# Building the experts' diagonal matrices on ScalarE instead of VectorE in a hybrid attention, DeltaNet and PEER block

## What is computed

```python
def peer(h, w_query, keys1, keys2, expert_down, expert_up):
    ...
        top_s, pos = lax.top_k(cand, PEER_TOPK)                 # 16 experts per head
        eidx = jnp.take_along_axis(cidx, pos, axis=-1)
        gates = jax.nn.softmax(top_s, axis=-1)
        u = expert_down[eidx]
        act = jax.nn.gelu(jnp.einsum('td,thkd->thk', xb, u).astype(jnp.float32), approximate=False)
        ve = expert_up[eidx]
        return jnp.einsum('thk,thkd->td', (gates * act).astype(xb.dtype), ve)
```

## Time and profile before

| | |
|---|---|
| device time, three runs | 2172.28, 2175.07, 2176.78 us; median 2175.07 |
| span of the profiled execution | 2172.1 us |
| before the first expert's dot | 0 to 493.5 us |
| experts of tiles 0 and 1, woven with the front | 493.5 to 1428.3 us |
| experts of tiles 2 and 3, alone | 1428.3 to 2154.7 us |
| busy: PE, DVE, ACT, POOL | 80%, 66%, 26%, 55% |
| moved from HBM | 649.84 MB |

### The profile page before, as it was taken

How to read it: one execution, slowest core, us unless ns; L and a number is a source line. 1 busy time by engine, 2 the same in 40 slices (tenths; PEclk the granted TensorE clock), 3 DMA queues, 4 the chain that set the end, 5 groups by cost and what they waited for, 6 DMA issues and landing times. The chain is left out here.

```text
span 2172.1 us, 23919 instructions
## 1 busy us (share of the span) xinstructions
PE 1742.9 (80%) x6788; PEld 1122.4 (52%) x6788; DVE 1431.1 (66%) x3407; ACT 558.1 (26%) x1222; POOL 1191.0 (55%) x1060
## 2 busy tenths in 40 slices
PE   7999999976878798787899868857777766777775
PEld 7888888864555475555666636522223322222222
DVE  0523322037788878888878787877677768677675
ACT  1522221021355427512333031121111111112111
POOL 2000000007656577566577667667777776777775
PEclk8999999988989899898999989989988997889988
DMA  8443234429989798788899999999999998999996
GB/s 295 130 139 119 79 117 136 146 87 355 399 280 330 281 407 316 250 299 275 294 409 394 408 326 404 379 344 366 368 358 365 382 366 333 371 368 371 360 380 242
DMA packets 178360, 653.16 MB, mean 301 GB/s; under 512 B 20096, under 2 KB 20304, under 8 KB 177504
## 3 DMA queue, kind: packets, MB, share of 16 engines
q0 software_dynamic: 148112, 541.77, 66.9%
q1 hardware_dynamic: 29952, 109.20, 14.5%
q10 hardware_dynamic: 208, 1.08, 0.1%
HBM read 649.84 MB, written 2.10 MB: 300 GB/s over the span
## 5 line engine op out<-in xcount | busy, mean ns | idle before, releaser
L1767 PE MATMUL PS<-pool_e,diag 128*128 128x512 f32 x1408 | 752.6, 677 | 324.9 <-DVE diag L1327 320.2
L589 POOL DMA_INDIRECT pool_e<-in_peer_u,idx x384 | 479.3, 1248 | 742.5 <-DVE idx L1306 473.2
L1767 PEld LDWEIGHTS PS<-pool_e,diag 128*128 128x128 f32 x1408 | 281.3, 212 | 710.2 <-issue 365.3
L589 POOL DMA_INDIRECT pool_e<-in_peer_v,idx x448 | 480.7, 1073 | 155.9 <-issue 125.6
L1350 DVE SCALAR_TENSOR_TENSOR pool_e<-pool_e,H 128x1024 f32<-128x1024 f32 x384 | 469.4, 1223 | 109.9 <-DMA pool_e<-in_peer_u,idx 97.9
L1481 PE MATMUL PS<-hT,ring 128*128 128x256 f32 x1792 | 407.1, 386 | 3.3 <-ACT hT L881 3.3
L1481 PEld LDWEIGHTS PS<-hT,ring 128*128 128x128 f32 x1792 | 348.3, 195 | 76.2 <-issue 29.7
L903 ACT ACTIVATE acts<-dots 128x1 f32<-128x1 f32 x256 | 51.4, 203 | 608.6 <-DVE pool_e L1350 299.6
L1327 DVE TENSOR_SCALAR diag<-ident,acts,wts 128x128 f32<-128x128 f32 x416 | 140.9, 345 | 3.7 <-ACT acts L909 3.6
L1350 DVE SCALAR_TENSOR_TENSOR gT<-gT,H 128x1024 f32<-128x1024 f32 x64 | 78.4, 1225 | 78.3 <-DMA gT<-in_peer_u,idx 77.1
L909 ACT ACT_TABLE_LOAD x59 | 75.7, 1283 | 184.5 <-DVE pool_e L1350 184.4
(11 more groups left out here) (323 smaller groups left out, 1907.0 us busy)
## 6 DMA issues: line engine op xcount, KB each, us to landing
ring<-in_w_tiles SPq DMA_DIRECT2D x200, 512.0 KB, 4.5
pool_e<-in_peer_v,idx POOLq DMA_INDIRECT x448, 6.3
pool_e<-in_peer_u,idx POOLq DMA_INDIRECT x384, 6.5
hT<-in_x_cols SPq DMA_DIRECT2D x2, 1024.0 KB, 8.3
mods<-in_ada_rows POOLq DMA_DIRECT2D x1, 2048.0 KB, 11.5
out_x<-X SPq DMA_DIRECT2D x4, 512.0 KB, 6.5
scores<-in_gain_rows POOLq DMA_DIRECT2D x1, 1536.0 KB, 15.9
X<-in_x_rows POOLq DMA_DIRECT2D x1, 1024.0 KB, 19.1
```

Of the source, the lines that this page charges most:

```text
L589: pool.indirect_dma_start(out=slot, out_offset=None, in_=table, in_offset=bass.IndirectOffsetOnAxis(ap=idx_sb[p][:, k:k + 1], axis=0),).th ...
L1767: ins = pe.matmul(PS[:, BANK_Y + half, :], diag[:, tile, :], rows[:, half * S:(half + 1) * S], start=False, stop=False, skip_group_check=True)
```

## The change

ACT makes the diagonal matrix. It applies gelu to (identity x dot), with the dot as a scale per token, and writes all 128x128 numbers into `diag` (gelu of 0 is 0, so only the diagonal remains); a second ACT instruction multiplies the matrix by the gate in place. For the experts that DVE adds up, ACT also makes the product of gelu and gate, one column at a time. DVE's `weigh` and the product in `add_up` are gone. Two semaphores are new: `wts_ready` (DVE to ACT: the gates of a head) and `act_ready` (ACT to DVE: the products). The wait for a free `diag` buffer (`e_free`) moves from DVE to ACT.

```diff
-LAG = (2, 2)
+LAG = 2
...
-            def gelu(head, p, k):
+            def gelu_of(p, k, tile):
+
+                act.activation(diag[:, tile, :], ident[:, :], ACT.Gelu, scale=dots[p][:, k:k + 1]).then_inc(gelu_ready, 1)
+
+            def gated_by(p, k, tile):
+
+                act.mul(diag[:, tile, :], diag[:, tile, :], wts[p][:, k:k + 1]).then_inc(diag_ready, 1)
+
+            def weigh_pair(h, k):
+
+                if k % 2 == 0:
+                    return
+                p = h % 2
+                if k == 1:
+                    act.wait_ge(wts_ready, h + 1)
+                for j in (k - 1, k):
+                    n = h * TOPK + j
+                    act.wait_ge(dot_ready, n + 1)
+                    if not added_by_pe(n):
+                        act.activation(acts[p][:, j:j + 1], dots[p][:, j:j + 1], ACT.Gelu).then_inc(gelu_ready, 1)
+                    else:
+                        m = count_pe(n)
+                        if m >= NDG:
+                            act.wait_ge(e_free, m + 1 - NDG)
+                        gelu_of(p, j, m % NDG)
+                for j in (k - 1, k):
+                    n = h * TOPK + j
+                    act.wait_ge(gelu_ready, n + 1)
+                    if added_by_pe(n):
+                        gated_by(p, j, count_pe(n) % NDG)
+                    else:
+                        act.mul(acts[p][:, j:j + 1], acts[p][:, j:j + 1], wts[p][:, j:j + 1]).then_inc(act_ready, 1)
+
+            def weigh(head, p, k):
+
                 act.wait_ge(dot_ready, head * TOPK + (k + 1))
-                act.activation(acts[p][:, k:k + 1], dots[p][:, k:k + 1], ACT.Gelu).then_inc(gelu_ready, 1)
-
-            def gelu_pair(h, k):
-
-                if k % 2:
-                    act.wait_ge(dot_ready, h * TOPK + k + 1)
-                    act.activation(acts[h % 2][:, k - 1:k + 1], dots[h % 2][:, k - 1:k + 1],
-                                   ACT.Gelu).then_inc(gelu_ready, 2)
+                act.wait_ge(e_free, head * TOPK + (k + 1 - NDG + LATER))
+                gelu_of(p, k, k % NDG)
+                act.wait_ge(gelu_ready, head * TOPK + (k + 1))
+                gated_by(p, k, k % NDG)
...
-                "expert": gelu_pair,
+                "expert": weigh_pair,
...
+                        act.wait_ge(wts_ready, head + 1)
+                        act.sem_inc(seen_act, 1)
                         for k in range(TOPK):
-                            gelu(head, p, k)
+                            weigh(head, p, k)
...
                 dve.tensor_scalar(wts[p][:, :], gate[p][:, 0:TOPK], gate[p][:, TOPK + 2:TOPK + 3], None,
-                                  ALU.mult)
+                                  ALU.mult).then_inc(wts_ready, 1)
                 dve.drain()
-
-            def weigh(head, p, k):
-
-                dve.wait_ge(gelu_ready, head * TOPK + (k + 1))
-                m = count_pe(head * TOPK + k) if isinstance(head, int) else k
-                if not isinstance(head, int):
-
-                    dve.wait_ge(e_free, head * TOPK + (k + 1 - NDG + LATER))
-                elif m >= NDG:
-                    dve.wait_ge(e_free, m + 1 - NDG)
-                dve.tensor_scalar(diag[:, m % NDG, :], ident[:, :], acts[p][:, k:k + 1],
-                                  wts[p][:, k:k + 1], ALU.mult, ALU.mult).then_inc(diag_ready, 1)
 
             def add_up(h, p, k):
...
-                dve.wait_ge(gelu_ready, n + 1)
-                link(dve.tensor_tensor(out=acts[p][:, k:k + 1], in0=acts[p][:, k:k + 1], in1=wts[p][:, k:k + 1],
-                                       op=ALU.mult))
+                dve.wait_ge(act_ready, n + 1 - count_pe(n + 1))
...
-                for m in behind(n, LAG[0]):
-                    (weigh if added_by_pe(m) else add_up)(m // TOPK, m // TOPK % 2, m % TOPK)
+                for m in behind(n, LAG):
+                    if not added_by_pe(m):
+                        add_up(m // TOPK, m // TOPK % 2, m % TOPK)
...
                             dot(p, k, u_slots[1][slot], h2)
-                            if k >= LAG[1]:
-                                weigh(head, p, k - LAG[1])
                             if k % 3 == 0 and k // 3 < 4:
 
                                 choose(1, ahead % HEADS if p else ahead, 1 - p, k // 3)
-                        for k in range(TOPK - LAG[1], TOPK):
-                            weigh(head, p, k)
```

More of the change, by code:

```diff
@@ L431, in hybrid_block @@
         gelu_ready = sem("gelu_ready")
+        act_ready = sem("act_ready")
+        wts_ready = sem("wts_ready")
         diag_ready = sem("diag_ready")
```

## The result

| | before | after |
|---|---|---|
| device time, median of 20 runs each | 2174.18 us | 2168.72 us (2148.11 to 2178.67) |
| ratio, 95% interval | | 0.9957 (0.9939 to 0.9976) |
| span of the profiled execution | 2172.1 us | 2168.3 us |
| first stretch (tiles 0 and 1, with the front), first dot to first dot | 934.8 us | 919.0 us |
| second stretch (tiles 2 and 3), first dot to last dot | 725.1 us | 737.7 us |

The change makes the kernel faster by 5.5 us, 0.4%, where 40 us were forecast; the time lies just above the range of 2095 to 2168. The direction was right and the size was not. The two stretches moved against each other: 15.8 us gained in the first, 12.6 us lost in the second.

The account below looks back on a forecast made before the run. POOL's queue of gathers was taken to bound the second stretch; DVE, row supply or ACT, by head, the first. Terms -25 - 9 + 4 + 4 - 5.5 - 9 = -40.5 gave 2135 us, range 2095 to 2168.

Parts of the forecast that it names:

- Starts of tiles: Second stretch, two tiles: ACT makes expert 0's matrix 2.8 us sooner, so PE starts earlier; -5.5 us.
- Table loads ahead of the wait: First stretch: ACT's table load moves before its wait for a dot, shortening the chain 0.85 us at 11 places; -9 us.
- DVE's relief: First stretch: 56.5 us of matrices and products leave DVE's queue, part of it kept; -25 us, bounds 0 and -56.
- the seven heads where DVE leads: First stretch: about seven of 16 heads (convolutions, DeltaNet, modulation before the scores) where DVE was said to set the pace.
- ACT's own work: First stretch: ACT's added instructions lengthen attention by 4 us and DeltaNet by 4 us; bounds for both 0 and +16.
- First stretch in all: First stretch: DVE's relief, Table loads ahead of the wait and ACT's own work taken together; -26 us.
- Gathers held by dots: Second stretch: without matrices between dots, 60 gathers that follow a held one run 0.15 us shorter; -9 us.
- Second stretch: Tiles 2 and 3: Starts of tiles and Gathers held by dots taken together; -14.5 us.
- signs of failure: Forecast wrong if DVE's or PE's waits for ACT pass 50 us, second stretch changes over 25, or first stays unchanged.
- Supply bound everywhere: Rival, both stretches: rows of u come no sooner however early buffers are free; 2166 us, chance 0.15.
- ScalarE becomes the bound: Rival, heads 5 to 9: ACT's added work delays PE's next stage and outweighs the relief; 2191 us, chance 0.10.
- The matrices held the gathers: Rival, second stretch: DVE's matrices cause the 86 us of held gathers; 2081 us, chance 0.09 shared with full relief kept.

Follow-up runs that it names:

- e8: Kernel before, with the first stretch's gelu of two columns split into two of one column, each with its own wait; 2165.9 us, ratio 0.9962.
- e9: Kernel before, with VectorE's 160 matrices and 96 products of the first stretch left out and made by nobody; 2162.7 us, ratio 0.9948.
- e10: Kernel before, with the edits of e8 and e9 together; 2148.7 us, ratio 0.9887.
- e1: Changed kernel with the second stretch put back, so the change is in the first stretch only; 2155.9 us, ratio 0.9901.
- the repeat: The changed kernel measured again, unaltered, against the kernel before; 2170.1 us, ratio 0.9963.
- e4: Kernel before, with the second stretch's dots reading the token row from PSUM in place of SBUF; 2110.8 us, ratio 0.9691.
- e7: e1 with the second stretch's dots reading the token row from PSUM in place of SBUF; 2091.9 us, ratio 0.9603.

## Where the prediction was right, and where it failed

- **Starts of tiles** (-5.5): right in mechanism, not timed alone. 2.55 us a tile on PE's start; POOL's 6.73 us became 4.94 (about 4 was forecast), and all its waits for PE and DVE 14.0 us in place of 26.0.
- **Table loads ahead of the wait** (-9): right in mechanism, too large in size. e8 gives 6.5 to 8 us for the load alone; the -9 had ScalarE's second gelu and multiplications on the chain already taken off (0.85 us saved of the 1.40), and those are not in e8. In the whole change 1.40 became 0.71 at the place shown. L1085's wait fell only from 12.2 to 8.1, not below 4; the gain shows in the heads, not in that row.
- **DVE's relief** (-25, "kept in the seven heads where DVE leads"): too large. Alone it is worth 16.7 us in the profile and 12 in time (e9), with PE released early as well. The step that failed in the first stretch is the split by heads: a head in which DVE is busiest is not one in which all of its relief is kept, since what it waits for next is a row of u or a result of PE. Heads 1 to 3 kept theirs (59.0, 72.6 and 72.9 us became 55.0, 68.5 and 69.8, so 11 of the 17); heads 6 to 9 kept 1 us together.
- **ACT's own work** (+8, bounds 0 and 16): about 13 by e10's one profile, about 3 by the times, both inside the bounds. It falls only in part where it was placed: 4 us in heads 5 to 9 (2.7 in the attention head 6, e1 against e10), but 6.5 in heads 0 to 3; of that the prediction had only what stands on the chain of the convolutions, inside the term above. First stretch in all: -26 forecast, -15.8 measured.
- **Gathers held by dots** (-9, bounds -86 and +10): this is where the forecast broke, with the wrong sign and outside its bounds. Held time rose by 19.6 us, in the repeat by 25.5. The working followed one gather behind one held gather and stopped at the pair; that part was right (12 us saved where 9 were forecast). It did not ask under what the next gathers start once the dots close up, though the bound of +10 named just that ("dots and gathers fall together more often"). It took each meeting as independent, in a stretch where POOL sets the pace and each held gather shifts all that follow. The other 24 + 10 us, more gathers just behind the start of a dot, it did not have; why there are more is open.
- **Second stretch** as a whole: -14.5 forecast, +12.6 measured. The signs of failure that the prediction named (waits for ACT above 50 us, a change above 25 us) were too coarse to catch this; the mean gather, forecast at 1.10 and found at 1.159, was the one that did. Of the other signs, DVE's busy time there fell by 65 us and not by 87, because a matrix of 0.34 us overlaps the dots and adds only 0.26, which the same prediction had used in its relief term; its waits for u rows grew by 79 us, as forecast.
- **Rivals.** "Supply bound everywhere" gave nearly the time (2166), but by another way: the first stretch did shrink by 16 us, and the second was not unchanged. "ScalarE becomes the bound" did not come: ACT is busy 38%, and the changed kernel is faster. "The matrices held the gathers" is refuted: in e4 and e7 DVE makes them all, and held time is 1.2 and 0.5 us. The Trainium skill (SBUF — State Buffer, "Who interferes with whom") says that `tensor_scalar` can take both ports; this form of it, 128x128 float32, is not seen to hold a gather in any run here. What decides the stretch is the hold by two SBUF inputs, which the prediction had read off but had not made a rival of.

## What to carry to other kernels

When an instruction leaves a queue, what stays behind closes up; if that is an operation with two SBUF inputs, look at what GpSimd issues in that time before counting the gain. In a stretch in which one queue is the bound and each of its steps may be held by another engine, small shifts can move the time by more than the work saved, and the same edit can cost nothing or 12 us depending on what runs before it: watch the mean duration of the step, and test with an idle instruction before believing any mechanism. Better, remove the hold: one operand in PSUM was worth 3% here, seven times the change under study.

## What the runs showed of the hardware

- A gather issued by GpSimd that starts under a VectorE operation with two inputs in SBUF ends 0.8 us behind that operation's end, 1.99 us in all in the row shown, against 0.94. With one of the inputs in PSUM it is not held: 497 gathers at a mean of 0.948 us, the dot itself no slower (1.22 us).
- VectorE `tensor_scalar` on 32 columns of float32 held its queue for 0.21 us and on 128 columns for 0.26: the width hardly matters at this size.
- The pattern between two engines was worth more here than the work in it: fillers that add 256 instructions took 0.6 to 1.4% off the changed kernel, and 112 of them, behind odd dots, 1.6% (ratios 0.9900, 0.9826 and 0.9800 against 0.9957 and 0.9963).
- `tensor_scalar` of 128x128 float32 on VectorE holds no gather: 72 (e4) and 86 (e7) gathers started under one and took 0.954 and 0.950 us on average.
- A table load (1.28 us) can stand on either side of a wait. With one gelu of two columns it was compiled behind the wait for the dot: in the first stretch of the kernel before, 50 of 59 such loads start right after an idle that a dot ended. With two gelus of one column (e8) none does, for 8 us of 2174.
